# Fifteen instead of eleven expert units loaded ahead of each expert stage

## What is computed

```python
N_GROUPS, EXP_PER_GROUP, N_EXPERTS, TOP_K, D_EXPERT = 4, 8, 32, 2, 512
...
x = layer_norm(DEEPNORM_ALPHA * x + (1 + gt_m) * y, ln_g[l, 0], ln_b[l, 0])
h = x * (1 + sc_f) + sh_f
y = hier_moe(h, moe_wgrp[l], moe_bgrp[l], moe_wexp[l], moe_bexp[l],
             moe_wgate[l], moe_wup[l], moe_wdown[l])
x = layer_norm(DEEPNORM_ALPHA * x + (1 + gt_f) * y, ln_g[l, 1], ln_b[l, 1])
...
def one_block(args):      # one expert e on the tokens xb routed to it
    xb, e = args
    hb = jax.nn.silu(xb @ w_gate[e]) * (xb @ w_up[e])
    return hb @ w_down[e]
```

## Time and profile before

| | us |
|---|---|
| median of three runs | 2657.39 |
| lowest, highest | 2653.95, 2661.37 |
| span of the profiled execution | 2656.2 |
| PE busy in it | 2450.2 (92%) |
| DVE busy | 1291.0 (49%) |
| ACT busy | 736.4 (28%) |
| DMA rate over the span | 260 GB/s, 690.77 MB |
| first expert stage (first expert matmul to last down matmul) | 1461.0 to 1929.2 |
| second expert stage | 2169.1 to 2636.8 |

### The profile page before, as it was taken

How to read it: one execution, slowest core, us unless ns; L and a number is a source line. 1 busy time by engine, 2 the same in 40 slices (tenths; PEclk the granted TensorE clock), 3 DMA queues, 4 the chain that set the end, 5 groups by cost and what they waited for, 6 DMA issues and landing times. The chain is left out here.

```text
span 2656.2 us, 40656 instructions
## 1 busy us (share of the span) xinstructions
PE 2450.2 (92%) x16214; PEld 1713.2 (64%) x16214; DVE 1291.0 (49%) x2016; ACT 736.4 (28%) x1086; POOL 157.2 (6%) x250
## 2 busy tenths in 40 slices
PE   8999999999998899999998999899888899999896
PEld 7998789989997799944885343333367653343332
DVE  7864468746875576445564321222266552222223
ACT  4334443334334433312221111111033521111111
POOL 1100001000110010020240000000000000000000
PEclk9999889999999899989998999999998999999998
DMA  8865238754873175433004899999953159999996
GB/s 336 309 236 181 74 123 311 277 191 175 316 277 127 64 271 212 166 130 131 33 4 153 360 423 423 424 423 424 422 191 133 48 215 423 423 423 424 423 424 280
DMA packets 110172, 690.77 MB, mean 260 GB/s; under 512 B 15760, under 2 KB 17104, under 8 KB 35168
## 3 DMA queue, kind: packets, MB, share of 16 engines
q1 hardware_dynamic: 88720, 618.10, 59.0%
q0 software_dynamic: 20320, 70.85, 7.2%
q10 hardware_dynamic: 1008, 0.06, 0.0%
HBM read 687.85 MB, written 1.11 MB: 259 GB/s over the span
## 5 line engine op out<-in xcount | busy, mean ns | idle before, releaser
L737 PE MATMUL bank<-ring,B 128*64 128x512 f32 (+1 forms) x1728 | 548.1, 597 | 59.9 <-DMA ring<-in_moe_wgate 59.9
L2045 DVE TENSOR_TENSOR ring_r<-ring,B_r 128x2048 fp32r<-128x2048 f32 x184 | 417.8, 2289 | 273.1 <-ACT B_r L1592 272.9
L737 PE MATMUL bank<-B_r 128*128 128x512 f32 (+1 forms) x1992 | 534.0, 353 | 13.8 <-DVE B_r L2382 6.0
L1592 ACT ACTIVATE B_r<-ring 128x2048 fp32r<-128x2048 f32 x184 | 347.0, 1909 | 293.7 <-PE bank L737 290.6
L737 PEld LDWEIGHTS bank<-B_r 128*128 128x128 f32 x1992 | 344.9, 193 | 111.3 <-issue 50.7
L737 PE MATMUL bank<-xt_r,B_r 128*128 128x256 f32 x1408 | 399.8, 284 | 5.4 <-DVE xt_r L2026 2.5
L737 PE MATMUL bank<-xt_r,ring_r 128*128 128x256 f32 x1408 | 398.4, 283 | 0.0
L737 PEld LDWEIGHTS bank<-ring,B 128*64 128x64 f32 (+1 forms) x1728 | 183.9, 143 | 325.1 <-issue 315.4
L737 PE MATMUL bank<-B 64*64 64x64 f32 (+7 forms) x2528 | 244.8, 289 | 38.8 <-DMA rows<-in_moe_wup 19.0
L737 PEld LDWEIGHTS bank<-xt_r,B_r 128*128 128x128 f32 x1408 | 269.9, 192 | 8.0 <-issue 5.2
L737 PEld LDWEIGHTS bank<-xt_r,ring_r 128*128 128x128 f32 x1408 | 269.9, 192 | 0.0
(11 more groups left out here) (361 smaller groups left out, 2895.8 us busy)
## 6 DMA issues: line engine op xcount, KB each, us to landing
ring<-in_moe_wgate SPq DMA_DIRECT2D x128, 1024.0 KB, 23.4
rows<-in_moe_wup SPq DMA_DIRECT2D x64, 1024.0 KB, 24.8
wks<-in_moe_wdown SPq DMA_DIRECT2D x64, 1024.0 KB, 23.1
ring<-in_ffn_w_gate SPq DMA_DIRECT2D x44, 1024.0 KB, 4.9
ring<-in_ffn_w_up SPq DMA_DIRECT2D x44, 1024.0 KB, 7.4
ring<-in_ffn_w_down SPq DMA_DIRECT2D x44, 1024.0 KB, 7.4
wks<-in_ada_w POOLq DMA_DIRECT2D x72, 512.0 KB, 6.1
ring<-in_moe_wup SPq DMA_DIRECT2D x32, 1024.0 KB, 22.7
```

Source lines behind the costliest of these rows:

```text
L737: ins = pe.matmul(out, lhsT, rhs, start=start, stop=stop, skip_group_check=True)
L1592: act.activation(hi, ring[:, slot, :], ACT.Copy).then_inc(sp_hi, 1)
L2045: dve.tensor_tensor(ring_r[:, slot, :], ring[:, slot, :], f32(hi), ALU.subtract).then_inc(sp_lo, 1)
```

## The change

It has these parts:

- Three units of the first two pairs are loaded to homes that are used once: `ONCE = (7, 11, 20)`, the last up unit and the last down unit of the first pair and the first down unit of the second, to B[7], B[1] and to the second half of B[4] with the first half of B[5] (`B4_B5`). They have semaphores of their own (`once_landed`) and don't count in `w_free`, so that a stage has 189 counted units (`EXPERT_UNITS`), and `begin_experts` sets the turn back to 0 for the second stage.
- The unit on the twelfth turn (a ring slot) waits for `pos - MORE`, that is for the last unit before the stage. With the twelve homes that makes units 0 to 13 and 20 loadable before PE's first expert matmul.
- SP issues the opening in another order, as homes come free: in stage 0 all six further homes and two of those used once when the source of `y_r` is ready, in stage 1 four and one when the attention output is, and the others when the projection is done; B[1] last, after the norm in front of the router. All other loads then wait for `pos - MORE`.
- `Yacc`'s memset is gone; the first four `add_blocks` of a stage copy instead of adding. `ye_lo` moves within B[5], `m_g4` and `m_slot` to B[4].
- `ln_b1`, `ln_b3` and the small loads wait for other counts of `w_free`, as the home they use is now the third and second last counted unit.
- `c` and the constants share the semaphore `const_landed`, on which ACT, PE, DVE and POOL wait for 32; POOL uses one chain semaphore for all its chains.

```diff
 MORE, MORE_AT = 6, 5
+ONCE = (7, 11, 20)
 UNIT = 2048
 BANK = 512
 NEG = -1.0e30
...
+    def begin_experts(self):
+
+        self.turn = 0
+
     def take_expert(self):
...
             self.take(dmas)
-        for _ in range(12 * PAIRS):
+        for _ in range(EXPERT_UNITS):
             self.take_expert()
     @contextmanager
...
-MOE_AT = [SPLIT_AT["kv_f"] + 20, SPLIT_AT["kv_f"] + 20 + 12 * PAIRS + 20]
+EXPERT_UNITS = 12 * PAIRS - len(ONCE)
+MOE_AT = [SPLIT_AT["kv_f"] + 20, SPLIT_AT["kv_f"] + 20 + EXPERT_UNITS + 20]
 PROJ_N = {n: k for n, k, _ in PROJ}
 TRANS_AT = {n: i for i, n in enumerate(TRANS)}
...
+        once = [B[7][:].rearrange("p a b -> p (a b)"), B[1][:].rearrange("p a b -> p (a b)"),
+                nc.alloc_sbuf_tensor_at("B4_B5", [P, UNIT], F32, offset=place["B4"] + 4 * D)[:]]
+
         def panel(slot):
             return ring[:, slot, :] if slot < R else more[slot - R]
...
         m_hot = Br[3][:, D + BANK:2 * D].rearrange("p (t s) -> p t s", t=TB)
-        ye_hi, ye_lo = Br[9][:, 0:D], Br[5][:, 0:D]
+        ye_hi, ye_lo = Br[9][:, 0:D], Br[5][:, D:2 * D]
         m_hotT = [Br[9][:, D + BANK * i:D + BANK * (i + 1)] for i in range(2)]
-        m_g4 = B[5][:, 1, 0:8].rearrange("p (t e) -> p t e", t=TB)
-        m_slot = [B[5][:, 1, 8 + 2 * i:10 + 2 * i] for i in range(2)]
         _r, _at = B[4][:, 0, :], [0]
         def rt(n, *shape):
...
         rt_cnt = rt(2)
+        m_g4, m_slot = rt(8, TB), [rt(2) for _ in range(2)]
         ov_flag = [sb(f"ov_flag{l}", [P, 1], I32) for l in range(LAYERS)]
         ov_h = m_h, m_sg
         ov_hT = m_hT, B[2][:, 0, 0:BANK]
...
@@ -682,23 +688,63 @@
                 g = A["moe_wgate_2"][l].rearrange("(i e) (p u k) n -> i e u p (k n)", e=2, u=2, p=P)
                 u = A["moe_wup_2"][l].rearrange("(i e) (p u k) n -> i e u p (k n)", e=2, u=2, p=P)
                 d = A["moe_wdown_2"][l].rearrange("(i e) (p u c) n -> i e u p (c n)", e=2, u=2, p=P)
-                def load_pair(i, first):
-
-                    for w in (g, u, d):
-                        for half in range(2):
-                            for e in range(2):
-                                slot, _, pos = cur.take_expert()
-                                if not first:
-                                    sp.wait_ge(w_free, pos - MORE)
-                                elif slot < R:
-                                    sp.wait_ge(w_free, pos)
-                                elif slot == R:
-                                    sp.wait_ge(pj_pe, PROJ_DONE[PROJ_AT[("wo_r", "wo_f")[l]] + 1] + TB)
-                                sp.dma_start(panel(slot), w[i, e, half]).then_inc(w_landed[slot], 16)
-
-                load_pair(0, True)
-                with cur.loop(sp, PAIRS - 1, R + MORE, R + MORE) as i:
-                    load_pair(i + 1, False)
+                def source(i, n):
+                    return (g, u, d)[n // 4][i, n % 2, n % 4 // 2]
+
+                def load_next(i, n):
+
+                    slot, _, pos = cur.take_expert()
+                    sp.wait_ge(w_free, pos - MORE)
+                    sp.dma_start(panel(slot), source(i, n)).then_inc(w_landed[slot], 16)
+
+                opening = [n for n in range(24) if n not in ONCE]
+                cur.begin_experts()
+                place_of = [cur.take_expert() for _ in range(R + MORE)]
+
+                def open_slot(t):
+
+                    slot, _, _ = place_of[t]
+                    i, n = divmod(opening[t], 12)
+                    sp.dma_start(panel(slot), source(i, n)).then_inc(w_landed[slot], 16)
+
+                def open_ring(t):
+
+                    pos = place_of[t][2]
+                    sp.wait_ge(w_free, pos if t < MORE_AT else pos - MORE)
+                    open_slot(t)
+
+                def open_once(x):
+
+                    i, n = divmod(ONCE[x], 12)
+                    sp.dma_start(once[x], source(i, n)).then_inc(once_landed[x], 16)
+
+                for t in (0, 1):
+                    open_ring(t)
+                if l == 0:
+                    sp.wait_ge(tr_src, TRANS_AT["y_r"] + 1)
+                    for t in range(MORE_AT, MORE_AT + MORE):
+                        open_slot(t)
+                    open_once(0)
+                    open_once(2)
+                else:
+                    sp.wait_ge(at_o, H // 4 * 3)
+                    for x in (0, 1, 2, 4):
+                        open_slot(MORE_AT + x)
+                    open_once(2)
+                for t in (2, 3, 4, MORE_AT + MORE):
+                    open_ring(t)
+                if l:
+                    sp.wait_ge(pj_pe, PROJ_DONE[PROJ_AT["wo_f"] + 1] + TB)
+                    for x in (3, 5):
+                        open_slot(MORE_AT + x)
+                    open_once(0)
+                sp.wait_ge(tr_src, TRANS_AT[f"moe{l}"] + 1)
+                open_once(1)
+                for n in opening[R + MORE:]:
+                    load_next(1, n - 12)
+                with cur.loop(sp, PAIRS - 2, R + MORE, R + MORE) as i:
+                    for n in range(12):
+                        load_next(i + 2, n)
                 w = [x.rearrange("i e u p q -> (i e) p u q") for x in (g, u, d)]
                 with overflowed(sp, l):
...
@@ -1013,18 +1059,28 @@
                         mm(o, w[:, t * P:(t + 1) * P], ye_hi[:, c], True, False)
                         mm(o, w[:, t * P:(t + 1) * P], ye_lo[:, c], False, True, signal=mo_s)
-            def expert_unit():
-
+            def expert_unit(opening, n):
+
+                if opening and n in ONCE:
+                    x = ONCE.index(n)
+                    pe.wait_ge(once_landed[x], 16 * opening)
+                    return once[x]
                 slot, landed, _ = cur.take_expert()
                 pe.wait_ge(w_landed[slot], landed)
                 return panel(slot)
-            def quad(n, i=None, first=False, last=False):
-
-                pair(n, 0, i, first, last)
-                pair(n + 1, 1, i, False, last)
-
-            def pair(n, j, i, first, last):
+            def quad(n, i=None, opening=0, last=False):
+
+                pair(n, 0, i, opening, last)
+                pair(n + 1, 1, i, opening, last)
+
+            def pair(n, j, i, opening, last):
+
+                first = opening and j == 0
+
+                def freed(u):
+
+                    return not (opening and 12 * j + u in ONCE)
                 def at(per, c):
...
+                        s = [expert_unit(opening, 12 * j + u + e) for e in range(2)]
                         for k in range(4):
                             for e in range(2):
                                 w = s[e].rearrange("p (k n) -> p k n", k=4)
                                 kk = 4 * half + k
                                 sig = None
                                 if k == 3:
-                                    sig = mo_gu if half and e else w_free
+                                    sig = mo_gu if half and e else w_free if freed(u + e) else None
                                 c = j * P + CAP * e
                                 mm(bank[x][CAP * e:CAP * (e + 1), :], xe[:, kk, c:c + CAP], w[:, k, :],
                                    kk == 0, kk == KC - 1, signal=sig)
-                    owed[0] += 1
+                    owed[0] += freed(4 * x + 3)
                     if x == 0 and not first:
                         pe.wait_ge(mo_ye, at(2, 0))
                         pe.wait_ge(mo_yl, at(2, 0))
...
                                 if c and d:
-                                    sig = mo_y if half and e else w_free
+                                    sig = mo_y if half and e else w_free if freed(u + e) else None
                                 mm(bank[2 + d][64 * e:64 * e + 64, :],
                                    m_hT[:, cc * P + 64 * e:cc * P + 64 * e + 64], w[:, c, d * BANK:(d + 1) * BANK],
                                    cc == 0, cc == 3, signal=sig)
-                owed[0] += 1
+                owed[0] += freed(11)
             def unpacked(l, i):
...
                     turn(j, bank[2 + j])
-                quad(n, first=True)
-                assert cur.pos == MOE_AT[l] + 24
+                cur.begin_experts()
+                quad(n, opening=l + 1)
+                assert cur.pos == MOE_AT[l] + 24 - len(ONCE)
                 with cur.loop(pe, PAIRS // 4 - 1, 48, R + MORE) as i:
                     quad(n + 2, i)
                     quad(n + 4, i)
...
             split(hi_up(0))
-            act.wait_ge(c_landed, 16)
+            act.wait_ge(const_landed, 32)
             act.activation(cs, cs, ACT.Silu).then_inc(cs_set, 1)
             ffn(0)
             split(hi_proj(0), 2)
...
@@ -2325,12 +2384,13 @@
                     dve.wait_ge(mo_x, v)
                     shifted(f"moe{l}", xe, c, o).then_inc(mo_xd, 1)
-                def add_blocks(wait):
+                def add_blocks(wait, begin):
                     for t in range(TB):
                         for e in range(2):
```

(33 more changed lines are left out.)

7 lines of the change are left out of this document (1 added, 6 removed).

## The result

| | before | changed |
|---|---|---|
| median, us | 2657.38 (4 runs) | 2643.53 (4 runs) |
| lowest to highest, us | 2653.95 to 2661.37 | 2636.24 to 2646.30 |
| span of the profiled execution, us | 2656.2 | 2634.5 |
| mean granted clock of PE | 0.961 | 0.957 |

The ratio is 0.9943, with a 95% interval of 0.9923 to 0.9963. The changed kernel is faster, by 14 us (0.6%) where 31 were forecast; 2643.5 lies above the upper end of the range, 2640.

A forecast was written before the change was run, and what follows sets the result against it. The DMA stream was taken to bound both expert stages; per stage 6.9 (restart) + 9.9 (fewer units) - 1.3 (rows) = 15.5 us, 31.0 for both, giving 2626 us, with an 8-in-10 range of 2616 to 2640.

The forecast's parts named there:

- Bound and stage lengths: Both expert stages are bound by the DMA stream and get 15.5 us shorter each.
- Restart: Expert stages: first load behind the opening comes 3.6 us after PE's first expert matmul, not 10.6, saving 6.9 us a stage.
- No gaps in the early stream: Behind the restart, loads issued as slots come free cost 0, with DMA at 424 GB/s; upper bound 12 us a stage.
- Units and rows: Expert stages: four units fewer to stream save 9.9 us, row loads cost 1.3; with the old restart, 8.6 a stage.
- PE's first stop for a landing: In the expert stage PE first waits for a load near pair 7, about 1640, no longer at 1512.
- The row behind stage 1: Its issue moves from 2622.00 to about 2631.8, landing 7 us before the final norm needs it; saves 1.2 us.
- everything after hangs on that, so both count in full: 31.0 us.: Both expert stages end on a down unit's landing, so their savings shorten the whole kernel by 31.0 us.
- The rivals: Expert stages: early loads paying latency (0.14), more gain than the sum (0.10), no lead (0.06), slower PE clock (0.04).
- The one on TensorE's clock: In the denser expert stages PE's granted clock falls from 2.4 to 1.2 GHz, giving 2715 us; chance 0.04.

The follow-up runs named there:

- gaps filled: Changed kernel with useless PE matmuls in its idle stretches before and early in the forgetting attention: 2633.56 us, ratio 0.9906.
- with 3 and 6 matmuls: Kernel before with three or six useless PE matmuls between stage 0's last scatter and the next transposes: 2656.28 us (ratio 1.0006) and 2652.94 us (1.0001).
- with 5 copies: Kernel before with five needless DVE copies of one block of shifted transposes behind stage 0: 2664.08 us, ratio 1.0027.
- with 1, 2, 4 matmuls: Changed kernel with one, two or four useless PE matmuls between stage 0's last scatter and the next transposes: 2634.72, 2622.36 and 2627.79 us.
- with 2 copies: Changed kernel with two needless DVE copies of one block of shifted transposes behind stage 0: 2625.17 us, ratio 0.9899.
- with fill elsewhere: Changed kernel with two useless matmuls behind stage 0 and useless matmuls in the two earlier attentions: 2629.24 us, ratio 0.9907.
- changed again: Changed kernel run once more without an edit: 2646.01 us, ratio 0.9957 to the kernel before.
- restart alone: Changed kernel without the three homes used once, keeping the twelfth turn's earlier wait and the early issue order: 2643.0 us, ratio 0.9950.
- homes alone: Changed kernel with the homes used once, but the twelfth turn again waiting for the sixth freed unit: 2655.94 us, ratio 0.9972.
- before with 4 copies: Kernel before with four needless DVE copies of one block of shifted transposes behind stage 0: 2664.83 us, ratio 1.0035.

## Why the forecast failed

One mark separates all profiles in which the gaps were left open. It is the length of the group of 16 matmuls behind the 2.81 us stop. With the gaps filled it takes 1.62 us, all at the full clock; the longer it takes, the sooner the clock fell in it:

| kernels | group of 16, us | 28 matmuls then take, us |
|---|---|---|
| before, and with 3 and 6 matmuls, with 5 copies | 2.41, 2.27, 2.47, 2.33 | 3.17 |
| changed with 1, 2, 4 matmuls, with 2 copies, with fill elsewhere | 2.53, 2.36, 2.40, 2.31, 2.27 | 3.17 |
| changed, changed again, restart alone, homes alone | 2.03, 2.05, 2.01, 1.97 | 5.84 |
| before with 4 copies | 2.01 | 5.84 |

Nine profiles with 2.27 us or more regained the clock at once, five with 2.05 or less did not; nothing lies between. The Trainium skill (TensorE: Matmul & The Clock Gate, "What's actually happening") says that what watches TensorE's activity runs free and isn't reset by the program; the runs agree, since about 1 us of DVE work far ahead of the loop decides about 15 us in it. The same section has the low clock as the default and activity as what releases it. Here PE was 100% busy from 2078 to 2110 in the kernel before with four copies, and its granted clock stayed at 0.50.

Why the changed kernel falls on the bad side in both its profiles, and before on the good one, stays open. It is no fixed moment of the program. The two profiles of the changed kernel reach the group of 16 at 2049.75 and 2058.37 us, and both lose. The length of stage 0 doesn't tell it (455.2, 456.6, 463.5, 465.3 and 471.3 us lose, 455.0 and 471.2 keep), nor does the way from the last scatter to the group (141.3 and 140.8 us in the two that lose, 141.3 with two copies, which keeps). What the two sides differ in is where in the group the clock falls, and what makes this so alike in executions of one kernel isn't shown. Nor is it shown why a slightly later fall is followed by four iterations more at the low clock.

Point by point, by the prediction's own steps:

- **Bound and stage lengths.** Right: 15.5 a stage forecast, 16.0 and 14.7 measured (14.6 and 13.9 in the second profile).
- **Restart.** Right. SP issues the first load behind the opening 3.65 us behind PE's first expert matmul, in stage 1 too (2161.89 and 2165.54), where it was 10.6; alone, with one unit more and the two rows in the stream, it is worth 5.9 and 6.8 us, against 6.9:

```profile
1456.86 1.99 SPq L698 DMA_DIRECT2D ring<-in_moe_wgate  x2
1460.30 3.76 SPq L698 DMA_DIRECT2D ring<-in_moe_wup  x3
...
2165.54 0.81 SPq L698 DMA_DIRECT2D ring<-in_moe_wgate  x2
```

- **No gaps in the early stream.** Right: 415 and 426 GB/s from 1460 to 1480, against 424 in the earlier trace rows. The Trainium skill (SBUF — State Buffer, "The DMA setup-cost knee") gives 330 to 340 GB/s for a transfer of 1 MiB. That isn't seen here, with loads issued in twos and threes.
- **Units and rows.** With the early restart taken out, 7.7 and 7.1 us against 8.6: the term was 0.9 to 1.5 us too high.
- **PE's first stop for a landing.** 1614.38, 161 us into the stage, where about 179 was forecast. The stage no longer ends on a down unit's landing as in the earlier trace rows: PE's last stop for DMA is at 1891.82 for an up unit. Neither cost anything that shows.
- **The row behind stage 1.** Right, if 2 us later than forecast. It goes out 5.9 us ahead of the last scatter (17.8 before; 8.0 forecast; the unit it waits for, the first down unit of the last pair, is the fourth last of those counted and not the third last), and the final norm doesn't wait for it: 16.6 us behind the last scatter against 16.4. POOL's timeline:

```profile
2611.96 0.53 POOL L3034 DMA_DIRECT2D rows<-in_ln_b  x1 [444.68 <-PE bank L783]
```

- **"... everything after hangs on that, so both count in full: 31.0 us."** This is the step that failed. What lies between the stages was taken as a block of fixed length that is merely moved. It isn't: it contains a loop that takes 3.76 or 7.05 us an iteration, by where the clock falls in front of it. In the changed kernel the stretch took 253.5 us where it had taken 236.9. 31.0 less these 16.6 is 14.4, and the medians show 14.
- **The rivals.** The one on TensorE's clock named the right mechanism and put it in the wrong place. It was priced inside the stages, where PE is dense and indeed kept 1.00, and dismissed because the fall had come behind idle time. The idle time is in front of the attention's loop, in a stretch in which the change leaves PE's matmuls as they were. The price of one matmul there could have been read from the kernel before, whose group of 14 took 2.93 us at the low clock; how many iterations would stay at it could not.

## What to carry to other kernels

A gain in one stage moves all that comes after it against the clock's own changes. Before counting it in full, look in the stretch behind it for places where the granted clock falls and recovers within a few iterations: whether it recovers can hang on 1 us of arrival, and a tuned kernel may sit on the good side by its timing alone. Look at the single times, not only the median: half of the executions may lose and half not. Measure the stages one by one; when their sum isn't in the total, compare windows with the clock. And try a small delay or a filled gap before giving up a change, or crediting it.

## What the hardware showed

- PE fully busy with small float32 matmuls (64 x 128) and transposes for 32 us stayed at 1.2 GHz (0.50 in the window from 2078 to 2110), while the same instructions ran at 2.4 GHz in nine other profiles.
- Work that does nothing made a kernel faster: about 0.9 us of matmuls, some 140 us ahead of a loop, brought the ratio to before from 0.996 to 0.984 (2646 and 2622 us, on two chips), about 1 us of DVE copies to 0.990 (2625 us, on a third).
- A stream of 1 MB loads moved 415 GB/s from 3 to 13 us behind the issue of its first load (1456.86), with slots coming free in twos and threes.
- The same edit in the kernel before and in the changed one need not have the same value: the fill of the attention was worth 0 in the one and 12 us in the other.
